# Which expert rows VectorE adds itself and which TensorE adds, in the last stage of a two-block network

## The reference

```python
def block(hb):                                   # 128 tokens at a time
    ...                                          # scores, then top 16 of 128 x 128 keys, 8 heads
    gates = jax.nn.softmax(top_s, axis=-1)
    u = expert_down[experts]                     # 8 x 16 = 128 experts for each token
    vv = expert_up[experts]
    act = jax.nn.gelu(jnp.einsum("thkd,td->thk", u, hb, ...), approximate=False)
    return jnp.einsum("thk,thkd->td", (gates * act).astype(vv.dtype), vv)
```

## Time and profile before

| | |
|---|---|
| median of 3 runs | 3529.98 us (3528.19 to 3537.58) |
| the profiled execution | 3529.98 us |
| its span (first to last instruction) | 3527.6 us, so 2.4 us lie around it |
| TensorE matmul busy | 3017.7 us |
| VectorE busy | 2139.1 us |
| ScalarE busy | 1392.4 us |
| GpSimd busy | 602.7 us |
| gathered bytes | 536.90 MB in 512 gathers |
| other loads | 251.69 MB on the weights' queue |

### The profile page before, as it was taken

How to read it: one execution, slowest core, us unless ns; L and a number is a source line. 1 busy time by engine, 2 the same in 40 slices (tenths; PEclk the granted TensorE clock), 3 DMA queues, 4 the chain that set the end, 5 groups by cost and what they waited for, 6 DMA issues and landing times.

```text
span 3527.6 us, 34722 instructions
## 1 busy us (share of the span) xinstructions
PE 3017.7 (86%) x12066; PEld 2089.0 (59%) x12066; DVE 2139.1 (61%) x3994; ACT 1392.4 (39%) x2876; POOL 602.7 (17%) x540
## 2 busy tenths in 40 slices
PE   5989999799777889999888978987879787777777
PEld 4867888587555668888667854465546432223222
DVE  6655443676455544442265479988867979755555
ACT  3233222444344433222473245865334343333333
POOL 0000000000000000000000003234544354443442
PEclk9999999899888999999899989999989899999999
DMA  6544444244111224444220449799999999999998
GB/s 222 185 137 126 143 140 143 77 136 125 36 36 47 84 85 143 141 143 123 96 90 19 140 184 361 287 356 353 402 420 419 356 420 421 421 421 421 421 421 342
DMA packets 147550, 797.84 MB, mean 226 GB/s; under 512 B 16305, under 2 KB 18481, under 8 KB 81713
## 3 DMA queue, kind: packets, MB, share of 16 engines
q0 software_dynamic: 73728, 536.90, 37.5%
q1 hardware_dynamic: 69840, 251.69, 22.0%
q10 hardware_dynamic: 3808, 7.02, 0.5%
HBM read 793.46 MB, written 2.10 MB: 226 GB/s over the span
## 4 chain that ended last, share of the span: by engine, by line
PE 55%; DMA 19%; DVE 17%; ACT 5%; issue 4%; POOL 0%; DVEq 0%; SPq 0%; ACTq 0%; POOLq 0%
PE psum L153 54%; DMA tail<-in_experts,tail 18%; DVE tail L187 4%; DVE tail L170 2%; ACT arena L164 2%; DVE tail L182 2%; DVE arena L182 2%; ACT L164 1%; DVE tail L193 1%; DVE tail L190 1%; ACT tail L164 1%; DVE region L170 1%; DVE tail L205 1%; DVE tail L196 1%; PE psum L158 1%
## 5 line engine op out<-in xcount | busy, mean ns | idle before, releaser
L153 PE MATMUL psum<-tail,arena 128*128 128x256 f32 (+2 forms) x3580 | 1267.9, 503 | 267.1 <-ACT arena L164 234.4
L153 PE MATMUL psum<-rounded,rounded 128*128 128x512 f32 x5496 | 1293.3, 396 | 40.5 <-DVE rounded L182 27.7
L153 PEld LDWEIGHTS psum<-rounded,rounded 128*128 128x128 f32 x5496 | 1036.5, 190 | 280.5 <-issue 56.4
L153 PEld LDWEIGHTS psum<-tail,arena 128*128 128x128 f32 x3580 | 672.1, 198 | 816.8 <-issue 759.3
L216 POOL DMA_INDIRECT tail<-in_experts,tail x512 | 582.6, 1138 | 1756.1 <-DVE tail L199 862.8
L187 DVE CUSTOM_DVE_ANT_0 tail<-tail 128x1024 f32<-128x1024 f32 x512 | 621.0, 1224 | 307.0 <-DMA tail<-in_experts,tail 300.8
L164 ACT ACTIVATE tail<-tail 128x1 f32<-128x1 f32 (+1 forms) x1056 | 266.9, 253 | 777.1 <-DVE tail L187 739.9
L170 DVE TENSOR_TENSOR rounded<-arena,rounded 128x1024 fp32r<-128x1024 f32 (+2 forms) x285 | 316.5, 1111 | 346.6 <-ACT rounded L164 346.5
L164 ACT ACTIVATE rounded<-arena 128x1024 fp32r<-128x1024 f32 (+2 forms) x317 | 292.0, 939 | 446.0 <-DVE arena L170 238.8
L153 PE MATMUL psum<-arena 128*128 128x1 f32 (+3 forms) x792 | 197.8, 375 | 87.3 <-ACT arena L164 47.5
L164 ACT ACTIVATE arena<-psum 128x256 f32<-128x256 f32 (+2 forms) x210 | 97.7, 481 | 419.5 <-PE psum L153 418.6
(11 more groups left out here) (82 smaller groups left out, 1567.0 us busy)
## 6 DMA issues: line engine op xcount, KB each, us to landing
arena<-in_ada SPq DMA_DIRECT2D x136, 512.0 KB
arena<-in_fin SPq DMA_DIRECT2D x88, 512.0 KB
arena<-in_win SPq DMA_DIRECT2D x56, 512.0 KB
arena<-in_fout SPq DMA_DIRECT2D x32, 512.0 KB
arena<-in_mxbc SPq DMA_DIRECT2D x32, 512.0 KB
arena<-in_pq SPq DMA_DIRECT2D x32, 512.0 KB
arena<-in_ain SPq DMA_DIRECT2D x24, 512.0 KB
arena<-in_mz SPq DMA_DIRECT2D x16, 512.0 KB
```

The costliest lines, as they stand in the source:

```text
L153: return self.e.matmul(o, a, b, start=start, stop=stop, skip_group_check=skip)
```

## The change

Only `own_add` differs:

```diff
         def own_add(n):
 
             s = n % 128
-            if n < 192:
-                return s % 2 == 1 and (16 <= s if n >= 128 else 48 <= s < 124)
-            return 16 <= s < 124 and s % (8 if n < 256 else 16) == 1
+            return 24 <= s < 124 and (s % 2 == 1 if n < 256 else s % 16 == 9)
```

## The result

The changed kernel takes 3556.22 us (median of 5 runs, 3555.14 to 3566.03), the kernel before 3533.34 us (median of 5, 3528.19 to 3537.58). The ratio is 1.0072, 95% interval 1.0056 to 1.0088: 20 to 31 us slower, about 25 us by the ratio. I had forecast 3560.0, 30.0 us more, in a range of 3543 to 3573.

A forecast was written before the change was run, and what follows sets the result against it. The prediction took the gathers' transfer rate to bound the end, with VectorE leaving the DMA idle in two earlier stretches. 14.4 + 15.6 = 30.0 us on a span of 3527.6, plus 2.4 around it, gave 3560.0 us, range 3543 to 3573.

The forecast's parts named there:

- What bounds the kernel: The kernel's end is the end of the gathers at transfer rate; DMA idle earlier is paid one for one.
- Who paces the two stretches: At 2170.5 to 2256.8 and 2699 to 2819.5 us VectorE paces, with 0.4 and 0.7 us of waits.
- Rival A: TensorE or the slots pace the gathers, so relieving them saves time: 3493 us, 4 in 100.
- The first group: Odd turns 25 to 47: 12 additions move to VectorE, which has no idle time, 12 x 1.20 = 14.4 us lost.
- rival B: The first stretch's 14.4 us are absorbed by TensorE's queue behind it: 3545.6 us, 12 in 100.
- The second group: Odd turns 195 to 227: 13 new VectorE additions cost 15.6 us; 9 more at 229 to 251 cost 0 to 3.
- The four turns given back: Odd turns 145 to 151 return to TensorE where DMA is full: worth 0, at most 7.8 us lost.
- blocks 2 and 3: The same 7 turns of each block, moved by 8 where the DMA is full: nothing.
- The sum: Whole kernel: 14.4 + 15.6 = 30.0 us more, giving 3560.0 us.
- the case of the sum: The main case, both costs arriving in full: 3560.0 us, bounds 3552 to 3567, 65 in 100.
- Rival C: TensorE's clock falls with less work, slowing its chain behind the first stretch by 9.8 us: 3570 us, 12 in 100.
- What I said would be seen: Signs: turns 24 to 47 and 195 to 227 longer at lower rates, 48 to 194 unchanged, TensorE's additions sooner behind diagonals.

The follow-up runs named there:

- e3: Kernel before, but from turn 324 on every odd turn (s 24 to 123) is added by VectorE, 68 additions more: 3529.66 us, ratio 1.0001.
- e1: Kernel before, with only the 12 odd turns 25 to 47 moved from TensorE to VectorE: 3542.14 us against 3529.46, ratio 1.0033.
- e2: Kernel before, with only the odd turns 193 to 251 of block 1 all VectorE's, 22 more additions: 3545.67 us, ratio 1.0045.
- e5: Kernel before, with turns 201, 209, 217 and 225 given back to TensorE: 3526.14 us against 3529.62, ratio 0.9993.
- e4: Kernel before, with the additions of the 12 odd turns 25 to 47 left out on both engines: 3530.34 us, ratio 0.9999.
- e8: Kernel before, with the 13 additions of odd turns 195 to 227 that the change moves left out altogether: 3530.88 us, ratio 1.0006.
- e10: The changed kernel run again, on the same chip as e9: 3559.05 us against 3530.94 for the kernel before, ratio 1.0082.
- e9: Kernel before, with odd turns 25 to 47 and 193 to 251 moved to VectorE, which keeps turns 145 to 151: 3558.04 us against 3530.94, ratio 1.0079.
- e11: Kernel before, with no VectorE additions in turns 195 to 232 and only every fourth in 100 to 127, 6 fewer: 3531.67 us, ratio 1.0000.

## Why the prediction was right, point by point

*What bounds the kernel.* Shown. e3 gives VectorE 68 additions at no cost where the DMA is full; e1 and e2 show that what VectorE's queue loses in the other two stretches arrives at the end: 12.5 us in the stretch and 11.6 in the time, 13.2 and 15.9.

*Who paces the two stretches.* Shown for both. VectorE's added work lengthens them, and its absence shortens the one in which I tried it (e5), while work left out of TensorE changes nothing (e4, e8). Rival A, which GpSimd's 65.5 us of waits spoke for, is refuted. The wait was real. That it ended so late because TensorE's additions stand behind main steps that wait for VectorE is argued from the order of the program; what e4 and e8 show is that freeing TensorE and slots shortens nothing.

*The first group, forecast 14.4 us.* The mechanism was right and the size 2 us too large: 12.6 us in its stretch, 12.5 in e1. Two things were missing, both in the term 12 x 1.20. A block's first addition on VectorE has nothing to add to: `dve_add` makes it a plain product. In e1 it stands here:

```profile
2177.75 0.75 DVE L176 TENSOR_SCALAR tail<-tail 128x1024 f32<-128x1024 f32 x1
2178.41 1.22 DVE L187 CUSTOM_DVE_ANT_0 tail<-tail 128x1024 f32<-128x1024 f32 x1
```

which is 0.66 us of the queue, not 1.20; in exchange turn 49, which had this form before, became a full addition. And turn 47's addition comes behind turn 48's dot product. Up to there that makes 0.66 + 10 x 1.20 = 12.7 us. The rest, 1.2 + 0.5 us, fell on the turns 48 to 57, where the kernel before had small waits of VectorE for TensorE (in the brackets):

```profile
2260.94 0.48 DVE L177 TENSOR_SCALAR tail<-psum,tail 128x256 f32<-128x256 f32 x1 [0.89 <-PE psum L158]
...
2267.01 0.48 DVE L177 TENSOR_SCALAR tail<-psum,tail 128x256 f32<-128x256 f32 x1 [0.73 <-PE psum L158]
```

and the same instructions in e1 have none:

```profile
2272.97 0.48 DVE L177 TENSOR_SCALAR tail<-psum,tail 128x256 f32<-128x256 f32 x1
...
2278.86 0.48 DVE L177 TENSOR_SCALAR tail<-psum,tail 128x256 f32<-128x256 f32 x1
```

So rival B was there, with 1.6 us instead of 14.4 (the two waits, 0.89 and 0.73).

*The second group, forecast 15.6 us and 0 to 3 behind it.* 13.4 us within the stretch and 3.1 behind (13.1 and 3.4 in e10). Twelve of the 13 additions come before turn 228's dot product, 14.4 us; about 1 us of them is hidden in waits of the kernel before, which the forecast took the stretch to be free of. About 0.4 us went between the turns 196 and 197, where VectorE waited for gathers, and about 0.8 behind turn 225, in the steps at the end of the ranking, where the wait for ScalarE shown above shrank from 2.1 to 1.7 us. The 3.1 behind hold the 13th, 1.2 us. The rest is no larger than what differs there anyway: e4, with the additions of before, takes 55.3 us for the turns 228 to 255, e5 and e8 take 55.6 and 56.4, and the change 56.1. So the 9 later additions cost little, as forecast, and how much stays open, as does what makes the traces differ there.

*The four turns given back, and blocks 2 and 3: forecast nothing.* e9 beside e10 shows no cost that these runs can tell.

*The sum.* Forecast 30.0 us; by stretches the change's trace has 12.6 - 0.1 + 0.1 - 0.1 + 0.8 + 13.4 + 3.1 = 29.8 and e10's 27.8. The times say 25.4 (interval 20 to 31) and 29.0 (24 to 34). That 29.8 lies so close to 30.0 is in part luck: both groups were forecast about 2 us too large for their stretches, and the turns 228 to 255, taken as 0, brought 3.1, of which up to 2.3 may be the difference between two traces. One bound was also set wrongly: a third of one stretch's cost is about 5 us, not the 8 by which the case of the sum goes down.

*Rival C, the clock.* The premise came true and the loss did not. In the first stretch the granted clock fell from 0.90 to 0.73, and to 0.71 in e1. In the turns 48 to 63 behind it, TensorE's chain, it was 0.96 in the changed kernel and 0.99 in e1, and they took 57.3 and 56.7 us, against 57.4 before. In the first stretch TensorE's products did get slower, 0.83 us for one MATMUL of an addition on average where the kernel before has 0.66, but VectorE paces it, and the clock was back behind it. The Trainium skill's page "TensorE: Matmul & The Clock Gate", section on oscillation, says that pauses between groups of products put the engine back to half its clock. The traces agree for the first stretch, 0.73 with 29.9 us of waits for VectorE and 0.90 with 12.5, and show no price of it in the kernel's time.

*What I said would be seen.* About 101 us and 250 GB/s for the turns 24 to 47: 98.8 and 253. About 136 us at 330 to 340 GB/s for 195 to 227: 134.1 and 333. 442 us for the turns 48 to 194: 443.3, and 442.6 before. TensorE's additions sooner behind their diagonals: for the even turns, start to start and on average, this was right in the later stretch, 2.3 us before and 0.7 after, and wrong in the first, 4.0 and 5.1. There TensorE waits longer for VectorE, 29.9 us for 12.5.

## What to carry to other kernels

Where the end is set by a stream of transfers, look for the stretches in which the stream is not full, and ask in each which engine has no waits at all. Work moved onto that engine costs nearly its full length (12.6 us for 14.4 here), and the same work costs nothing where the stream is full. A long wait for an engine does not say that this engine sets the pace: leave its work out once, and see whether the stretch gets shorter. And where two engines are nearly balanced, taking work from the full one gains little or loses: in e11 it lost 4.5 us.

## What the runs showed of the hardware

The granted clock of TensorE was lower in these stretches where it had less to do: 0.97 with 357.47 of 467.70 us busy, 0.79 with 288.19 of 466.10 (e3), and 0.73 with 58.14 of 86.30 (e4), means between the 1.2 and the 2.4 GHz level. The busy share alone does not order it. In the turns 228 to 255 it was 0.94 with 32.56 of 56.50 us busy in e10, and 0.80 with 36.63 of 55.80 in e9. Behind the cold first stretch it was again 0.96 to 1.00 in the 57 us that followed. I had not expected that a stretch so cold would leave no trace in the time.

GpSimd's instructions took longer beside a busier VectorE: in the stretch from turn 324 on, 179 gathers were busy for 238.66 us in e3 and for 185.09 before. The rate of the transfers stayed at 418 and 417 GB/s. What the two engines share is not shown.

The beginning of these programs has identical instructions, and turn 0 starts between 2073.7 and 2085.4 us in the 13 traces. That spread of 12 us is as large as the first group's whole effect, and it is why a single profiled execution should be compared stretch by stretch.
